# The second block's modulation summed on VectorE alone, with a seventh slot in the weight ring

## The chip, the cores and the metric

One Trainium2 chip, one core of it. The kernel is one launch; its time is the device time in microseconds (us) of that core, and the time of a kernel is the median of its runs.

## What is computed

A two-block network over 256 tokens of width 1024, all in float32. The first block has two layers, each of feed-forward, three attention branches and feed-forward; the second block has two layers with a Fourier or RWKV mixer and a mixture of 16 experts. Cut to what the change touches:

```
for l in range(2):                                   # first block
    x = x + 0.5 * swiglu(rmsnorm(x, g1[l]), w_ffn1_in[l], w_ffn1_out[l])
    x = x + merged_attention(x) @ w_out[l]
    x = x + 0.5 * swiglu(rmsnorm(x, g2[l]), w_ffn2_in[l], w_ffn2_out[l])
for i in range(2):                                   # second block
    mod_x   = silu(c)     @ ada_w[i] + ada_b[i]      # six parts of 1024 each
    mod_ctx = silu(c_ctx) @ ada_w[i] + ada_b[i]
    ... mixer(modulated x, ctx) ...; x = x + gate * ec_moe(modulated x)
```

The two modulation vectors depend on `c` and `c_ctx` alone, so the kernel computes them early, during the first block's feed-forward stages. `ada_w[i]` is 1024 x 6144: it is cut into three groups of 8 chunks of 128 x 2048.

## The kernel before

**The stream.** Nearly all weights are one stream of 632 chunks of 1 MB (128 partitions x 2048 float32, `CHUNK`), in the order of use. SyncE loads chunk c into slot c mod `RING` of the weight ring (`stream_weights`, L328 to L343). It loads a chunk as soon as the semaphore `chunks_used` says that the chunk `RING` places before it is used up; `RING` is 6. TensorE raises that semaphore after the last product with a chunk. ScalarE issues the other loads, some expert chunks among them ("kept" chunks, L2319).

**A feed-forward stage** (`ffn`, L601 on; four of them, stages 0, 2, 3 and 5). It has 33 weight chunks, numbered as pairs 0 to 32, each of two half-chunks i = 2 x pair and 2 x pair + 1. Half-chunks 0 to 43 are the up projection, in 11 groups of four; 44 (`UP`) to 65 are the down projection. For each half ScalarE rounds it to the high part (`round_half`, L644 to L650), VectorE subtracts to get the low part (`rest_half`, L652 to L655), and TensorE makes three products for each of two token tiles and two column blocks, 12 matmuls (L657 to L660). There are four split buffers, so half i is rounded once TensorE is done with half i - 4. After group n ScalarE applies SiLU, VectorE multiplies (`hid`, L877), TensorE transposes the result of the group before (`turn`, L693 to L702), ScalarE and VectorE save its high and low part (L830, L864). TensorE's order at the end of the up projection is: group 10, turn(9), halves 44 and 45 for token tile 1, turn(10), halves 44 and 45 for tile 0, then half by half. ScalarE's order there is: save(10), an activation table load (L853), then rounding of half 48 on.

**The modulation in these stages.** One group of `ada_w` for one stream (x or context) is weighed on VectorE: after each of the pairs 2, 4, ..., 16 the stream has one `ada` chunk, which VectorE multiplies by a column of silu(c) and adds to `partial_sums` (`weigh`, L672 to L682), in the program after the rest of half 2 x pair + 3. TensorE waits for that sum within the same half before it gives both chunks free (`follows_weighted`, `both_done`). At half UP + 15 `add_up` (L684 to L690) sums `partial_sums` over the partitions with four matmuls into bank 7. In stages 0, 2 and 3 a second group, for both streams at once, goes through TensorE: after pairs 25 and 29 the stream has four `ada` chunks, and `ada_chunk` (L1617 to L1623) makes four matmuls of 128 x 32 weights with each into bank 6. VectorE copies both banks out at half 64. In stage 0 GpSimd also places the attention bias (`place_bias`, L975 and L978).

**The expert stages** (`experts`, L1836 on; their products are L2103) follow a Fourier and an RWKV mixer. Each reads its own weights once, 16 experts of 12 chunks. Four chunks of an output projection (L1933) come before.

Of the kernel before, what the change touches and what calls it, by code (L numbers as in the profile page):

```python
# [17 lines left out]
F32 = mybir.dt.float32  # L18
F32R = mybir.dt.float32r
ALU = mybir.AluOpType  # L20
# [3 lines left out]
P = 128  # L24
# [9 lines left out]
CHUNK = 2048  # L34
RING = 6
HD = 64
# [24 lines left out]
class Signal:  # L61
# [10 lines left out]
    def dma(self):  # L72
        self.count += 16
        return self.sem, 16


# [107 lines left out]
class Program:  # L184
    def __init__(self, nc, io, ctx):
# [415 lines left out]
    def ffn(self, stage, second, ada=None, inner=None):  # L601
# [3 lines left out]
        with_bias = stage == 0  # L605
        split_fourth, hid_hi, hid_lo = self.scratch((CHUNK, F32R), (FT * SEQ, F32R), (FT * SEQ, F32R))
        hid_hi, hid_lo = (x[:, :].rearrange("p (k t) -> p k t", t=SEQ) for x in (hid_hi, hid_lo))
# [20 lines left out]

        group, stream = second
        weighted0, added0 = self.weighted.count, self.added_up.count  # L630

        def chunk_of(i):

            pair = i // 2
            return c0 + pair + min((pair - 1) // 2 if pair else 0, KT) + (min(max(pair - 2 * groups, 0) // 4 * 4, KT) if ada is not None else 0)

# [28 lines left out]
        def follows_weighted(i):  # L665
            return i % 4 == 3 and 7 <= i < 7 + 4 * KT

# [3 lines left out]

        def weigh(dve, k):  # L672
            self.wait_chunk(dve, chunk_of(4 * k + 7) - 1)
            if k == 0 and with_bias:
                dve.wait_ge(self.early["conditioned"].sem, 1)
            c, w = self.ada[:, 32 * k + stream:32 * k + stream + 1], self.slot(chunk_of(4 * k + 7) - 1)
            if k == 0:
                ins = dve.tensor_scalar(self.partial_sums[:, :], w, c, None, ALU.mult)
            else:
                dve.wait_ge(self.weighted.sem, weighted0 + k)  # L680
                ins = dve.scalar_tensor_tensor(out=self.partial_sums[:, :], in0=w, scalar=c, in1=self.partial_sums[:, :], op0=ALU.mult, op1=ALU.add)
            ins.then_inc(*self.weighted.up())  # L682

        def add_up(pe):  # L684
            pe.wait_ge(self.weighted.sem, weighted0 + KT)
            for j in range(4):
                last = pe.matmul(self.psum[32 * j:32 * j + 32, 7, :], self.pick[:, 1 - stream:33 - stream],
                                 self.partial_sums[:, j * NB:(j + 1) * NB], start=True, stop=True)
            last.then_inc(*self.added_up.up())

        @self.block.tensor
        def _(pe):
# [73 lines left out]
            for n in range(1, groups):  # L766
                if inner is not None:
                    inner.on_pe(pe, n - 1)
                if n >= 2:
                    pe.wait_ge(self.hid_done.sem, hid0 + n - 1)  # L770
                for i in range(4 * n, 4 * n + 4):
                    pe.wait_ge(self.rest.sem, rest0 + i + 1)
                    last = up(n, i, 0)
                    if follows_weighted(i):
                        pe.wait_ge(self.weighted.sem, weighted0 + n)
# [22 lines left out]
            for i in range(UP, N - 4):  # L798
                if i >= UP + AHEAD:
                    pe.wait_ge(self.rest.sem, rest0 + i + 1)  # L800
                    hidden(i)
                last = down(i, 0)
                if i >= UP + AHEAD:
                    last = down(i, 1)
                half_done(last, i)
                k = (i - UP) // 2
                if ada is not None and i == UP:
                    pe.wait_ge(self.early["conditioned"].sem, 1)
# [50 lines left out]
        def _(dve):  # L859
# [24 lines left out]
            for i in range(UP + 4, N):  # L884
                rest_half(dve, i)
                if i == N - 2:
                    dve.wait_ge(self.added_up.sem, added0 + 1)
# [5 lines left out]
                if ada is not None and i == N - 2:  # L893
                    dve.wait_ge(self.chunks_used.sem, chunk_of(UP + 2 * KT - 1) + 2)
                    dve.tensor_copy(self.ada_saved[ada], self.psum[:, 6, :]).then_inc(*ve.up())
# [719 lines left out]
    MOD = 34064  # L1615

    def ada_chunk(self, pe, chunk, k, cT, bank):  # L1617

        self.wait_chunk(pe, chunk)
        for j in range(4):  # L1620
            last = pe.matmul(self.psum[32 * j:32 * j + 32, bank, :], cT[:, k * 32:(k + 1) * 32],
                             self.slot(chunk)[:, j * NB:(j + 1) * NB], start=(k == 0), stop=(k == KT - 1))
        last.then_inc(*self.chunks_used.up())  # L1623

# [2096 lines left out]
def _stream(i):  # L3721
    parts = []
    ada = [_ada(i["ada_w_2"][l])[KT * g:KT * (g + 1)] for l in range(DEPTH) for g in range(3)]

    def up(w, group):
        for n, chunk in enumerate(_gate_up(w)):
# [4 lines left out]
    def down(w, group=None):  # L3731
        rows = list(_row_pairs(w))
        extra = [] if group is None else [ada[group][k - 3:k + 1] if k % 4 == 3 else ada[group][0:0] for k in range(KT)]
        for n, row in enumerate(rows):
            parts.append(row[None])
            parts.extend(extra[n:n + 1])

    for l in range(DEPTH):
        up(i["w_ffn1_in"][l], 5 if l else 4)
        down(i["w_ffn1_out"][l], 2 if l else 0)  # L3740
        parts += _mixer(i["w_in"][l], i["w_branch"][l], i["w_out"][l])
        up(i["w_ffn2_in"][l], 3)
        down(i["w_ffn2_out"][l], None if l else 1)
    for l in range(DEPTH):
# [117 lines left out]
```

## Time and profile before

| | us |
|---|---|
| three timed runs | 2948.0, 2947.13, 2941.61 |
| their median | 2947.13 |
| the profiled execution | 2939.34 |
| its span (first to last instruction) | 2937.5 |
| TensorE busy in the span | 2689.6 (92%) |
| VectorE busy | 1266.6 (43%) |
| ScalarE busy | 983.0 (33%) |
| mean DMA rate over the span | 244 GB/s |

The stretches of the span, in order: stage 0 to about 214 us, the attention stage, stage 2 from about 465, stage 3 from about 660, attention, stage 5 from about 1110 to 1300; the Fourier mixer to 1395; the first expert stage to about 1875; RWKV to about 2430; the second expert stage to the end. An engine's busy share says nothing alone: read for each stretch what is busy all through it, and what the engine next to finish last waits for. TensorE's ends in the profile are modelled; where two matmuls overlap in the timeline, the difference of their starts is the time that one takes.

### The profile page before, as it was taken

The numbers are of one execution on the slowest core, as the hardware profiler recorded it, in microseconds if no ns is written. First come the engines' busy times: TensorE is split into PE (matmuls) and PEld (weight loads), VectorE is DVE, ScalarE is ACT, GpSimd is POOL, SyncE is SP. The second block draws the span as 40 slices with busy tenths as digits, with TensorE's granted clock in tenths as the row PEclk, the third lists the DMA queues.
The fourth block names the chain that finished last, engine by engine and source line by source line (L and its number), as shares of the span: only waits on it lengthen the run. The fifth ranks groups of instructions, "written<-read, shape, count | busy, mean of one in ns | idle before, by whom it ended". The sixth has DMA issues, their size and how long they took to land. (4 is left out here: it accounts for less than half of the span.)

```text
span 2937.5 us, 56637 instructions
## 1 busy us (share of the span) xinstructions
PE 2689.6 (92%) x24326; PEld 1793.2 (61%) x24326; DVE 1266.6 (43%) x1829; ACT 983.0 (33%) x1704; POOL 189.1 (6%) x195
## 2 busy tenths in 40 slices
PE   8999999999999999999999998899999989776676
PEld 6877877878878878875433332344788864333332
DVE  5646566647556567643100001423777763000001
ACT  4435655434446555531200100202555542000000
POOL 0102000000002000000000000002343310000000
PEclk9999999999999999999999999999999989977777
DMA  7674335776673347633899999822000007999998
GB/s 302 244 283 163 126 131 213 269 287 244 247 283 129 129 163 274 229 136 113 347 421 421 421 421 421 331 85 74 33 17 11 11 21 305 421 421 421 417 421 337
DMA packets 103709, 715.43 MB, mean 244 GB/s; under 512 B 11916, under 2 KB 14348, under 8 KB 19512
## 3 DMA queue, kind: packets, MB, share of 16 engines
q1 hardware_dynamic: 93592, 667.94, 57.5%
q10 hardware_dynamic: 9888, 44.04, 4.0%
q8 instruction: 192, 3.15, 0.4%
q14 instruction: 37, 0.30, 0.0%
HBM read 710.86 MB, written 1.07 MB: 242 GB/s over the span
## 5 line engine op out<-in xcount | busy, mean ns | idle before, releaser
L2103 PE MATMUL banks<-weight_ring,scratch 128*32 128x256 f32 (+1 forms) x4304 | 567.1, 508 | 144.4 <-DMA weight_ring<-in_stream 142.7
L2103 PEld LDWEIGHTS banks<-weight_ring,scratch 128*32 128x32 f32 (+1 forms) x4304 | 185.9, 129 | 505.8 <-DMA weight_ring<-in_stream 252.7
L655 DVE TENSOR_TENSOR split_high<-weight_ring,split_high 128x1024 fp32r<-128x1024 f32 x198 | 244.5, 1243 | 207.6 <-ACT split_high L650 204.9
L650 ACT CAST split_high<-weight_ring 128x1024 fp32r<-128x1024 f32 x198 | 206.9, 1052 | 290.4 <-PE banks L660 218.7
L2254 DVE TENSOR_TENSOR scratch<-scratch,banks 128x512 f32<-128x512 f32 (+1 forms) x32 | 17.7, 554 | 570.4 <-PE banks L2103 570.4
L1433 DVE TENSOR_TENSOR split_high<-weight_ring,split_high 128x1024 fp32r<-128x1024 f32 x128 | 160.2, 1263 | 160.9 <-ACT split_high L1326 160.7
L658 PE MATMUL banks<-split_high,features_low 128*128 128x512 f32 x480 | 189.8, 395 | 0.0
L660 PE MATMUL banks<-split_high,features_high 128*128 128x512 f32 x480 | 187.1, 390 | 0.0
L659 PE MATMUL banks<-split_high,features_high 128*128 128x512 f32 x480 | 186.8, 389 | 0.0
L1326 ACT CAST split_high<-weight_ring 128x1024 fp32r<-128x1024 f32 x128 | 133.0, 1049 | 150.2 <-PE banks L1075 144.3
L2163 ACT ACTIVATE scratch<-banks 128x512 f32<-128x512 f32 (+1 forms) x32 | 15.7, 490 | 474.3 <-PE banks L2103 474.3
L1073 PE MATMUL banks<-split_high,features_low 128*128 128x512 f32 x392 | 156.6, 399 | 0.3
L1075 PE MATMUL banks<-split_high,features_high 128*128 128x512 f32 x392 | 152.9, 390 | 0.0
L1074 PE MATMUL banks<-split_high,features_high 128*128 128x512 f32 x392 | 152.9, 390 | 0.0
L2165 ACT COPY scratch<-banks 128x512 f32<-128x512 f32 (+1 forms) x32 | 15.3, 479 | 339.5 <-PE banks L2076 339.5
L655 DVE TENSOR_TENSOR scratch<-weight_ring,scratch 128x1024 fp32r<-128x1024 f32 x66 | 80.7, 1223 | 79.6 <-ACT scratch L650 79.1
L658 PE MATMUL banks<-split_high,scratch 128*128 128x512 f32 x264 | 103.6, 392 | 0.0
L660 PE MATMUL banks<-split_high,scratch 128*128 128x512 f32 x264 | 102.8, 389 | 0.0
L659 PE MATMUL banks<-split_high,scratch 128*128 128x512 f32 x264 | 102.7, 389 | 0.0
L650 ACT CAST scratch<-weight_ring 128x1024 fp32r<-128x1024 f32 x66 | 69.5, 1052 | 97.4 <-PE banks L660 59.7
L659 PEld LDWEIGHTS banks<-split_high,features_high 128*128 128x128 f32 x480 | 90.2, 188 | 19.0
L658 PEld LDWEIGHTS banks<-split_high,features_low 128*128 128x128 f32 x480 | 90.1, 188 | 18.9
(438 smaller groups left out, 4748.8 us busy)
## 6 DMA issues: line engine op xcount, KB each, us to landing
weight_ring<-in_stream SPq DMA_DIRECT2D x632, 1024.0 KB, 10.3
scratch<-in_kept ACTq DMA_DIRECT2D x20, 1024.0 KB, 9.6
scratch<-in_pair_rows ACTq DMA_DIRECT2D x8, 448.0 KB, 3.7
scratch<-in_kept ACTq DMA_DIRECT2D x6, 512.0 KB, 6.9
scratch<-in_lora ACTq DMA_DIRECT2D x2, 1536.0 KB, 8.4
front<-in_gain_rows ACTq DMA_DIRECT2D x5, 512.0 KB, 3.7
bias<-bias_rows SPq DMA_DIRECT2D x1, 2304.0 KB
scratch<-in_routing ACTq DMA_DIRECT2D x1, 1040.5 KB, 5.0
```

Source lines behind the costliest of these rows:

```text
L650: act.copy(split[i % 4][0], source(i)).then_inc(*self.rounded.up())
L655: dve.tensor_tensor(lo, source(i), hi.bitcast(F32), ALU.subtract).then_inc(*self.rest.up())
L658: pe.matmul(out, lhs_lo, hi, start=start, stop=False)
L659: pe.matmul(out, lhs_hi, lo, start=False, stop=False)
L660: return pe.matmul(out, lhs_hi, hi, start=False, stop=stop)
L1073: pe.matmul(out, lhs_lo, hi, start=start, stop=False)
L1074: pe.matmul(out, lhs_hi, lo, start=False, stop=False)
L1075: return pe.matmul(out, lhs_hi, hi, start=False, stop=stop)
L1326: act.copy(split[i % 3][0], source(i)).then_inc(*self.rounded.up())
L1433: dve.tensor_tensor(lo, source(i), hi.bitcast(F32), ALU.subtract).then_inc(*self.rest.up())
L2103: last = pe.matmul(self.psum[q * M:(q + 1) * M, (GATE, UP, DOWN)[part], 0:W], left, w[j][:, q * W:(q + 1) * W], start=(k == 0), stop=(k == ...
L2254: dve.tensor_tensor(hid[:, e % 2, 0:W], silu[:, e % 2, 0:W], self.psum[:, UP, 0:W], ALU.mult).then_inc(*up("hid"))
```

## The change

All three groups that went through TensorE are now weighed on VectorE too. In stages 0, 2 and 3 the stream has one chunk of that group after each of the pairs in `OWN_AT`: 13, 17, 19, 21 (up projection) and 23, 24, 26, 28 (down projection), and no bursts of four. For each, `weigh` makes two sums, one for each stream, one in the first half of `front` and one in the upper half of `resid`. `add_up` sums all three over the partitions (12 matmuls in these stages, 4 in stage 5), and stands after half 61 in all four stages instead of half 59. TensorE waits for the weighed sums in the middle of an up half and ahead of a down half. `partial_sums` moves into the stage's scratch, `flip` into a part of `ada`; the ring has seven slots; the Pool queue's scratch for dynamic DMAs goes from 1024 to 256 bytes.

```diff
-RING = 6
+RING = 7
+OWN_AT = (13, 17, 19, 21, 23, 24, 26, 28)
-        self.partial_sums = self.last.enter_context(nc.sbuf_tensor("partial_sums", [P, CHUNK], F32))
-        self.flip = self.resid[:, 3584:3712]
+        self.flip = self.ada[:, 1280:1408]
...
+        own_sums = [(self.front[:, 0:CHUNK], 0), (self.resid[:, 2 * D:4 * D], 1)]
+        weighted_at = {2 + 2 * k: (k, [(partial_sums[:, :], stream)]) for k in range(KT)}
+        if ada is not None:
+            weighted_at |= {place: (k, own_sums) for k, place in enumerate(OWN_AT)}
...
         def follows_weighted(i):
-            return i % 4 == 3 and 7 <= i < 7 + 4 * KT
+            return i % 2 == 1 and i // 2 - 1 in weighted_at
+
+        def weighted_by(i):
+            return weighted0 + sum(len(sums) for place, (_, sums) in weighted_at.items() if place < i // 2)
...
+            if k:
+                dve.wait_ge(self.weighted.sem, self.weighted.count)
+            for total, s in sums:
+                c, w = self.ada[:, 32 * k + s:32 * k + s + 1], self.slot(chunk)
+                if k == 0:
+                    ins = dve.tensor_scalar(total, w, c, None, ALU.mult)
+                else:
+                    ins = dve.scalar_tensor_tensor(out=total, in0=w, scalar=c, in1=total, op0=ALU.mult, op1=ALU.add)
+                ins.then_inc(*self.weighted.up())
 
         def add_up(pe):
-            pe.wait_ge(self.weighted.sem, weighted0 + KT)
+            pe.wait_ge(self.weighted.sem, weighted_by(N))
...
+            if ada is not None:
+                for total, s in own_sums:
+                    for j in range(4):
+                        out, cols = slice(32 * j, 32 * j + 32), slice(j * NB, (j + 1) * NB)
+                        last = pe.matmul(self.psum[out, 6, :], self.pick[:, 1 - s:33 - s], total[:, cols], start=(s == 0), stop=(s == 1))
...
+                if follows_weighted(i):
+                    pe.wait_ge(self.weighted.sem, weighted_by(i))
                 last = down(i, 0)
...
-                if ada is not None and i % 2 == 1 and k % 4 == 3 and k < KT:
-                    for j in range(4):
-                        self.ada_chunk(pe, chunk_of(i) + 1 + j, k - 3 + j, self.ada, 6)
-                if i == UP + 2 * KT - 1:
-                    add_up(pe)
+            add_up(pe)
...
                     rest_half(dve, i)
-                if n < KT:
-                    weigh(dve, n)
+                    if follows_weighted(i):
+                        weigh(dve, i)
...
-    nc = bacc.Bacc("TRN2", target_bir_lowering=False, num_devices=1, dynamic_dma_scratch_size=1024)
+    nc = bacc.Bacc("TRN2", target_bir_lowering=False, num_devices=1, dynamic_dma_scratch_size=256)
```

## Rows read from the trace of the kernel before

**Rows 1.** Page, parts 2, 3 and 4: rate in 40 slices, queues, chain.
```profile
GB/s 302 244 283 163 126 131 213 269 287 244 247 283 129 129 163 274 229 136 113 347 421 421 421 421 421 331 85 74 33 17 11 11 21 305 421 421 421 417 421 337
...
q1 hardware_dynamic: 93592, 667.94, 57.5%
q10 hardware_dynamic: 9888, 44.04, 4.0%
...
DMA 12%; PE 4%; DVE 1%; ACT 0%; issue 0%; SPq 0%; ACTq 0%; DVEq 0%
```

**Rows 2.** Windows: stretch, length, busy us (xcount) by engine, clock, DMA share, GB/s.
```profile
1395.00:1840.00 445.00, 413.82 (x2034) 155.17 (x2034) 47.44 (x105) 45.46 (x102) 0.00 (x0) 0.99 0.99 409
2430.00:2937.50 507.50, 371.64 (x3740) 174.99 (x3738) 51.81 (x127) 38.82 (x89) 0.00 (x0) 0.82 0.96 395
```

**Rows 3.** Windows of 10 us where both expert stages' first products begin.
```profile
1410.00:1420.00 10.00, 10.00 (x70) 8.76 (x70) 1.47 (x8) 5.08 (x14) 0.00 (x0) 0.83 0.47 138
...
2480.00:2490.00 10.00, 8.87 (x112) 6.53 (x116) 2.13 (x7) 4.71 (x10) 0.00 (x0) 1.00 0.23 77
```

**Rows 4.** Timeline of TensorE, first feed-forward stage: start, length, instructions.
```profile
173.61 0.39 PE L660 MATMUL banks<-scratch,scratch 128*128 128x512 f32 x1
173.92 3.64 PE L1621 MATMUL banks<-weight_ring,ada 128*32 128x512 f32 x32
177.50 0.50 PE L658 MATMUL banks<-split_high,scratch 128*128 128x512 f32 x1
...
199.16 0.39 PE L660 MATMUL banks<-scratch,scratch 128*128 128x512 f32 x1
...
202.94 1.04 PE L687 MATMUL banks<-partial_sums,small 128*32 128x512 f32 x8
203.91 0.50 PE L658 MATMUL banks<-split_high,scratch 128*128 128x512 f32 x1
```

**Rows 5.** Timeline of TensorE, fourth feed-forward stage, around its L687.
```profile
1273.66 0.39 PE L660 MATMUL banks<-split_high,scratch 128*128 128x512 f32 x1
...
1274.98 0.50 PE L658 MATMUL banks<-scratch,scratch 128*128 128x512 f32 x1
```

**Rows 6.** Instructions of L681: min/median/max ns, first and last start.
```profile
L681 DVE SCALAR_TENSOR_TENSOR partial_sums<-weight_ring,ada,partial_sums x28: 2342/2344/2347, 43.6 to 1196.8; 128x2048 f32<-128x2048 f32 x28
```

**Rows 7.** Timeline of VectorE, first feed-forward stage, its last two groups.
```profile
142.15 0.68 DVE L877 TENSOR_TENSOR front<-front,banks 128x512 f32<-128x512 f32 x1
...
146.94 1.23 DVE L655 TENSOR_TENSOR split_high<-weight_ring,split_high 128x1024 fp32r<-128x1024 f32 x1 [1.49 <-ACT split_high L650]
...
153.52 0.68 DVE L877 TENSOR_TENSOR front<-front,banks 128x512 f32<-128x512 f32 x1
```

**Rows 8.** Timeline of TensorE, same stage: the transposes of the last group.
```profile
154.29 0.62 PE L701 MATMUL banks<-ident,front 128*128 128x128 f32 x4
```

**Rows 9.** Timeline of ScalarE, same stage, after its last group.
```profile
155.55 1.28 ACT L853 ACT_TABLE_LOAD   x1
```

**Rows 10.** Timeline of VectorE, same stage: rests of half-chunks 48 to 51.
```profile
158.02 2.36 DVE L655 TENSOR_TENSOR split_high<-weight_ring,split_high 128x1024 fp32r<-128x1024 f32 x2 [1.77 <-ACT split_high L650]
...
161.52 1.23 DVE L655 TENSOR_TENSOR split_high<-weight_ring,split_high 128x1024 fp32r<-128x1024 f32 x1 [1.14 <-ACT split_high L650]
164.24 1.23 DVE L655 TENSOR_TENSOR scratch<-weight_ring,scratch 128x1024 fp32r<-128x1024 f32 x1 [1.49 <-ACT scratch L650]
```

**Rows 11.** Timeline of GpSimd, first feed-forward stage.
```profile
118.90 4.26 POOL L975 TENSOR_SCALAR_AFFINE_SELECT bias<-bias 128x3072 f32<-128x3072 f32 x1 [118.47 <-ACT bias L963]
123.31 3.60 POOL L978 TENSOR_SCALAR_AFFINE_SELECT bias<-bias 128x3072 f32<-128x3072 f32 x1
```

**Rows 12.** Timeline of VectorE over the same time.
```profile
118.16 2.34 DVE L681 SCALAR_TENSOR_TENSOR partial_sums<-weight_ring,ada,partial_sums 128x2048 f32<-128x2048 f32 x1
120.43 0.68 DVE L877 TENSOR_TENSOR front<-front,banks 128x512 f32<-128x512 f32 x1
...
121.63 7.49 DVE L655 TENSOR_TENSOR split_high<-weight_ring,split_high 128x1024 fp32r<-128x1024 f32 x3
```

More of the change, by code:

```diff
@@ L605, in ffn @@
         with_bias = stage == 0
-        split_fourth, hid_hi, hid_lo = self.scratch((CHUNK, F32R), (FT * SEQ, F32R), (FT * SEQ, F32R))
+        split_fourth, hid_hi, hid_lo, partial_sums = self.scratch((CHUNK, F32R), (FT * SEQ, F32R), (FT * SEQ, F32R), (CHUNK, F32))
         hid_hi, hid_lo = (x[:, :].rearrange("p (k t) -> p k t", t=SEQ) for x in (hid_hi, hid_lo))
@@ L634, in chunk_of @@
             pair = i // 2
-            return c0 + pair + min((pair - 1) // 2 if pair else 0, KT) + (min(max(pair - 2 * groups, 0) // 4 * 4, KT) if ada is not None else 0)
+            return c0 + pair + sum(place < pair for place in weighted_at)
         def used(i):
@@ L670, in both_done, with weigh @@
             ins.then_inc(self.chunks_used.sem, 2)
-        def weigh(dve, k):
-            self.wait_chunk(dve, chunk_of(4 * k + 7) - 1)
+        def weigh(dve, i):
+            k, sums = weighted_at[i // 2 - 1]
+            chunk = chunk_of(i) - 1
+            self.wait_chunk(dve, chunk)
             if k == 0 and with_bias:
[L675 to L682, printed above, removed]
+                if sums is own_sums:
+                    dve.wait_ge(self.bias_moved.sem, self.bias_moved.count)
+                else:
+                    dve.wait_ge(self.early["conditioned"].sem, 1)
+            if k:
[4 more added lines that the diff above has]
+                    ins = dve.tensor_scalar(total, w, c, None, ALU.mult)
+                else:
+                    ins = dve.scalar_tensor_tensor(out=total, in0=w, scalar=c, in1=total, op0=ALU.mult, op1=ALU.add)
+                ins.then_inc(*self.weighted.up())
@@ L684, in add_up @@
         def add_up(pe):
-            pe.wait_ge(self.weighted.sem, weighted0 + KT)
+            pe.wait_ge(self.weighted.sem, weighted_by(N))
             for j in range(4):
-                last = pe.matmul(self.psum[32 * j:32 * j + 32, 7, :], self.pick[:, 1 - stream:33 - stream],
-                                 self.partial_sums[:, j * NB:(j + 1) * NB], start=True, stop=True)
+                out, cols = slice(32 * j, 32 * j + 32), slice(j * NB, (j + 1) * NB)
+                last = pe.matmul(self.psum[out, 7, :], self.pick[:, 1 - stream:33 - stream], partial_sums[:, cols], start=True, stop=True)
@@ L801, in _ @@
                     hidden(i)
+                if follows_weighted(i):
+                    pe.wait_ge(self.weighted.sem, weighted_by(i))
                 last = down(i, 0)
@@ L804, in _ @@
                     last = down(i, 1)
[L805 to L808, printed above, removed]
-                if ada is not None and i % 2 == 1 and k % 4 == 3 and k < KT:
-                    for j in range(4):
-                        self.ada_chunk(pe, chunk_of(i) + 1 + j, k - 3 + j, self.ada, 6)
-                if i == UP + 2 * KT - 1:
-                    add_up(pe)
+                if follows_weighted(i):
+                    both_done(last)
+                else:
+                    half_done(last, i)
+            add_up(pe)
             for t in range(TT):
@@ L870, in _ @@
                     rest_half(dve, i)
-                if n < KT:
-                    weigh(dve, n)
+                    if follows_weighted(i):
+                        weigh(dve, i)
                 dve.wait_ge(self.act_done.sem, act0 + n + 1)
@@ L885, in _ @@
                 rest_half(dve, i)
+                if follows_weighted(i):
+                    weigh(dve, i)
                 if i == N - 2:
@@ L1615 @@
     MOD = 34064
[L1617 to L1623, printed above, removed]
     def copy_mod(self, dve, g, bank):
@@ L3723, in _stream, with feed @@
     ada = [_ada(i["ada_w_2"][l])[KT * g:KT * (g + 1)] for l in range(DEPTH) for g in range(3)]
-    def up(w, group):
-        for n, chunk in enumerate(_gate_up(w)):
+    def feed(w_in, w_out, group, own=None):
+        for n, chunk in enumerate([*_gate_up(w_in), *_row_pairs(w_out)]):
             parts.append(chunk[None])
@@ L3729, in up @@
                 parts.append(ada[group][n // 2 - 1:n // 2])
[L3731 to L3736, printed above, removed]
+            if own is not None and n in OWN_AT:
+                k = OWN_AT.index(n)
+                parts.append(ada[own][k:k + 1])
     for l in range(DEPTH):
-        up(i["w_ffn1_in"][l], 5 if l else 4)
-        down(i["w_ffn1_out"][l], 2 if l else 0)
+        feed(i["w_ffn1_in"][l], i["w_ffn1_out"][l], 5 if l else 4, 2 if l else 0)
         parts += _mixer(i["w_in"][l], i["w_branch"][l], i["w_out"][l])
-        up(i["w_ffn2_in"][l], 3)
-        down(i["w_ffn2_out"][l], None if l else 1)
+        feed(i["w_ffn2_in"][l], i["w_ffn2_out"][l], 3, None if l else 1)
     for l in range(DEPTH):
```

3 lines of the change are left out of this document (1 added, 2 removed).

## Prediction

> **What bounds the kernel now.** I read the page's chain and queues first, then the time by stretch, then the timelines where the edit acts. The chain of waits that ended last gives 12% of the span to DMA and 4% to TensorE [rows 1]; it reaches back only to the entry of the second expert stage, and so tells of that alone. The windows by stretch say the rest. In both expert stages the DMA engines are busy for 0.99 and 0.96 of the time at about 409 and 395 GB/s, while TensorE has idle time: 31 of 445 us and 136 of 507 us [rows 2]. There the weight stream sets the end. In the feed-forward stages it is the other way round. One matmul follows another without a gap in TensorE's timeline, the bursts included [rows 4], and the edit touches exactly these two kinds of stretch: matmuls in the one, prefetch in the other.
>
> **Part 1, the removed bursts.** In stages 0, 2 and 3, `ada_chunk` runs twice, four chunks at a time. The first burst is 32 records in 3.64 us, and the time that it really costs is the distance between the normal products around it: 177.50 - 173.61 = 3.89, less the 0.23 that lies between two such products anyway (12 of them in a half of 2.72 us, [rows 10]), so 3.66 us. The second burst with `add_up` behind it costs 203.91 - 199.16 - 0.23 = 4.52 [rows 4]. Together 8.18 us of TensorE time per stage, none of it beside other TensorE work, so all on the path.
>
> **Part 2, the larger `add_up`.** Where it stands alone, in stage 5, the old one of 4 matmuls costs 1274.98 - 1273.66 - 0.23 = 1.09 us [rows 5]; behind a burst, 203.91 - 202.94 = 0.97 [rows 4]. A set of four that follows others costs what the second burst takes beyond the first, 4.52 - 3.66 = 0.86. New price 1.09 + 2 x 0.86 = 2.81. So per stage 8.18 - 2.81 = 5.37 us less on TensorE. In stage 5 it only moves by two halves: nothing.
>
> **Part 3, the weighing.** A sum costs 2344 ns, and all 28 of them lie within 5 ns [rows 6]; the next instruction starts 2.27 us after it [rows 12]. One own chunk is 4.54 us on VectorE (in the first of each stage the sums are plain products, and shorter). In all 3 x 15 x 2.3 = some 105 us are added to VectorE, and TensorE shows none of it as long as each lies within the lead that the four split buffers give. That lead: TensorE takes 2.72 us for a half (rests 50 and 51 start at 161.52 and 164.24, [rows 10]). Half 51 ends at 173.84, where the burst begins [rows 4], so half 47 ended four halves earlier, at 162.96, and rest 51 started 1.28 us later. A rest ends 2.5 us after half i - 4 is done, while half i is wanted 3 x 2.72 = 8.16 us after. A rest then has 5.7 us to spare, and a weighing of 4.54 us in front of the wait for it leaves some 1.1 us. So single weighings (halves 29, 37, 41, 55, 59) are hidden, in the down projection barely; in the up projection TensorE waits half a half later (1.4 us more). Two places aren't like that.
>
> *The turn of the last group.* The chunk after pair 21 is weighed after rest 45. Rest 45 starts at 146.94, so the sums end at 146.94 + 1.14 + 4.54 = 152.62; rests 46 and 47 follow at 1.14 each (both have been rounded by then), and the product `hid` of group 10 starts at 154.90 instead of 153.52 [rows 7]. It takes 0.68 and a semaphore, so turn(10) can start at about 155.65. It starts at 154.29 now, right at the end of the present product: it has no slack [rows 8]. TensorE's order is fixed, so it waits: **1.36 us** per stage, three times.
>
> *Two chunks in a row.* The chunks after pairs 23 and 24 are weighed after rests 49 and 51. ScalarE's table load (now at 155.55, [rows 9]) moves with turn(10) by 1.36, and so do rests 48 and 49, which now start at 158.02 [rows 10]. VectorE then runs without a gap: rests 48, 49 from 159.38, sums to 166.2, rests 50, 51 to 168.5, sums to 173.1. TensorE wants the first pair of sums when half 48 is done, at 167.0 (162.96 + 2.72 + 1.36), which holds by 0.7, and the second when half 50 is, at 172.5: it waits **0.7 us**. After that each weighing has 1.1 us to spare again.
>
> Per stage 5.37 - 1.36 - 0.7 = 3.3, times three 9.8 us. Behind TensorE's new waits stand only its own next halves; behind VectorE's sums stand the rests, counted above. The chunk to be weighed lies in the stream ahead of the chunk whose rest was just made, so waiting for it costs nothing. The copies of banks 6 and 7 at half 64 wait for `add_up` after half 61: counted from the end of half 60 they end at 2.72 + 2.81 + 1.2 = 6.7 us, and rest 65 at 7.9; it is wanted at 5.53 + 3 x 1.36 = 9.6. Hidden by 1.7 us.
>
> **Part 4, GpSimd in stage 0.** While its two selects run, from 118.90 to 126.9 [rows 11], three rests that take 3.5 us elsewhere take 7.49 [rows 12]: 4 us lost. The own chunk after pair 17 is weighed right behind them. VectorE's work in a group of four is then 4 x 1.14 + 2 x 0.6 + 4.54 = 10.3 us against 11.37 for TensorE (142.15 to 153.52, [rows 7]), so it makes up about 1.07 a group; of the lateness about 0.5 us is left at turn(10). The bounds are 0 and 2 us. I take 0.5, so 9.3 for the stages. The Trainium skill (SBUF — State Buffer, section Who interferes with whom) says that a VectorE instruction with two SBUF inputs and a GpSimd one that reads SBUF exclude each other, whoever starts first. The trace agrees with it for the rests. By that rule the change would lose up to 7.9 us here if its sums fell on the selects; by the order of the rows they fall behind them, so the 0.5 stays.
>
> **Part 5, the seventh slot.** A chunk is 1.05 MB, and at 421 GB/s, the rate of the full slices, takes 2.49 us [rows 1]. At the start of the experts' products the ring is full and the DMA engines partly idle, 0.47 and 0.23 busy [rows 3], and later never again. So with seven slots one chunk more is in place when the stream becomes the bound, and the stage ends one transfer earlier: 2.49 us each, 5.0 together. It can't be more from this, since DMA has no gap left to fill after that; it can be nothing if TensorE, 93% busy in the first expert stage [rows 2], is its real bound. In the feed-forward stages the slot covers the denser stretch (pairs 12 to 17 and 21 to 28), where a half-pair of 5.4 us uses two chunks that take 5.0 to load: no gain, it keeps the supply.
>
> **Parts at nothing.** The scratch for dynamic DMAs: both busy queues are hardware ones, issued by SyncE and ScalarE [rows 1], none by GpSimd. The first seven loads delay the bias round trip on SyncE by one transfer, 2.5 us; the bias is first used in the third group, two groups of 11.37 us later. The moved buffers change no size.
>
> **Sum.** 9.3 + 5.0 = 14.3 us. Span 2937.5 to 2923.2, the profiled execution 2939.3 to 2925.0. The median of the runs lies 7.8 above that execution; against it the forecast is 2947.1 - 14.3 = **2932.8 us**.
>
> **Rivals.**
>
> *The two waits don't come* (the last product and turn have slack that I don't see, or a rest and a sum overlap more). Then 3 x 5.37 + 5.0 = 21.1: 2926.0. Against it: turn(10) starts now the moment `hid` is there. Chance 0.15.
>
> *The seventh slot gives nothing*, TensorE being the bound of the first expert stage and the second refilling as before: 9.3 alone, 2937.8. For it is 93% busy; against it the DMA rate without a dip. Chance 0.15.
>
> *VectorE is tighter than the rows add up to.* With 1.2 us more at turn(10) and at each of the weighings 49, 51, 55 and 59 (semaphores, a rounding that comes late because its chunk does) the stages lose 1.2 + 0.5 + 1.2 + 0.1 + 0.1 = 3.1 each, and give nothing: only the 5.0 of the ring is left, 2942.1. The lead of 1.1 us is small enough for it. Chance 0.15.
>
> *Slower: the weighing becomes the bound of the down projection.* Its place is halves 48 to 59, where VectorE has 4 x 2 sums and 12 rests: 8 x 2.27 + 12 x 1.14 = 31.8 us against 12 x 2.72 = 32.6 of TensorE. The point is 0.8 us: whatever VectorE needs beyond the rows there goes into the end. At 2.27 us a sum it holds; with a sum at 3.4 us, half as long again (a second operand from a slot that is being written, say), it's 8 x 1.1 - 0.8 = 8.2 more, and 2 more at turn(10), with 1.1 x 2 in each up-group that has no room: about 12 per stage, 36 - 14.3 = 22 slower: 2969; slower at all from a sum of 2.8 us. The 28 sums within 5 ns, all beside running loads, speak against it. Chance 0.07.
>
> The forecast as it stands has 0.48.
>
> **Range and chances.** The forecast with its own bounds (0 to 2 us for GpSimd, 0.5 us per wait, the scatter of the median, 6.4 us between the runs of before) is 2927 to 2939. To hold 8 in 10 it must take in the first rival and most of the third: 2923 to 2945. About 0.2% (5.9 us) is what a measurement of this kernel can tell from no change, so faster is below 2941.2. Forecast, first and second rival lie there but for the scatter, and a third of the third: 0.76. Same 0.16, slower 0.08.
>
> **What would show it.** In the profile after: no L1621; 24 matmul records at `add_up` within about 2.8 us; 45 sums more at 2.34 us; a wait of TensorE of about 1.4 us for L877's successor ahead of the last turn and of 0.7 us ahead of half 51, in each of three stages, and none at halves 55 and 59; the Fourier stage starting 9 us earlier, and each expert stage shorter by 2.5. If the waits are absent, part 3 was wrong about the lead; if the expert stages keep their length, part 5 was.

## The result and the profile after

| | before | after |
|---|---|---|
| median of the runs shown together | 2941.47 (2937.47 to 2948.0, 6 runs) | 2928.41 (2919.31 to 2930.3, 6 runs) |
| ratio after/before | | 0.9940, 95% interval 0.9927 to 0.9953 |
| the profiled execution | 2939.34 | 2928.78 |
| its span | 2937.5 | 2927.0 |

The changed kernel is faster: by 13 us if the two medians are subtracted, by 14 to 21 us if the interval of the ratio is taken. The forecast was 14.3 us. The ratio, here and below, is the one on record for each comparison, with its 95% interval. It isn't the quotient of the medians shown, which is 0.9956 here; in all comparisons but one the ratio lies 0.0003 to 0.0016 below that quotient (with five slots they agree). So a gain read from a ratio and one read from medians differ by up to 5 us. Run once more beside other runs of before, the changed kernel stood at 0.9946. Its page, busy time and chain:

```profile
span 2927.0 us, 56413 instructions
PE 2669.4 (91%) x24182; PEld 1787.8 (61%) x24182; DVE 1365.9 (47%) x1877; ACT 984.8 (34%) x1704; POOL 188.9 (6%) x195
...
DMA 12%; PE 4%; DVE 0%; ACT 0%; issue 0%; SPq 0%; ACTq 0%
```

VectorE is busy for 99 us more, TensorE for 20 us less, and the chain hasn't changed: it tells of the last stage alone, as [rows 1] did.

TensorE's timeline in the first feed-forward stage of after. Where [rows 4] had two bursts, there is one run of `add_up`; the transposes of the last group, turn(10) (L721 was L701), and half 51 now wait:

```profile
150.72 0.60 PE L721 MATMUL banks<-ident,front 128*128 128x128 f32 x4
...
155.59 0.66 PE L721 MATMUL banks<-ident,front 128*128 128x128 f32 x4 [1.51 <-DVE front L895]
...
172.22 0.39 PE L665 MATMUL banks<-split_high,scratch 128*128 128x512 f32 x1
173.19 0.47 PE L663 MATMUL banks<-scratch,scratch 128*128 128x512 f32 x1 [0.58 <-DVE resid L696]
...
203.01 0.39 PE L665 MATMUL banks<-split_high,scratch 128*128 128x512 f32 x1
203.32 1.07 PE L703 MATMUL banks<-scratch,small 128*32 128x512 f32 x8
204.21 1.04 PE L708 MATMUL banks<-front,small 128*32 128x512 f32 x8
205.06 1.04 PE L708 MATMUL banks<-resid,small 128*32 128x512 f32 x8
206.04 0.50 PE L663 MATMUL banks<-split_high,scratch 128*128 128x512 f32 x1
```

The bracket is the idle time before the instruction and what ended it. VectorE's timeline says why (L660 is the rest, L696 the sum, L895 `hid`):

```profile
148.06 2.34 DVE L696 SCALAR_TENSOR_TENSOR front<-weight_ring,ada,front 128x2048 f32<-128x2048 f32 x1
150.33 2.33 DVE L696 SCALAR_TENSOR_TENSOR resid<-weight_ring,ada,resid 128x2048 f32<-128x2048 f32 x1
...
154.86 0.67 DVE L895 TENSOR_TENSOR front<-front,banks 128x512 f32<-128x512 f32 x1
...
168.43 2.35 DVE L696 SCALAR_TENSOR_TENSOR front<-weight_ring,ada,front 128x2048 f32<-128x2048 f32 x1
170.69 2.35 DVE L696 SCALAR_TENSOR_TENSOR resid<-weight_ring,ada,resid 128x2048 f32<-128x2048 f32 x1
```

`hid` starts at 154.86 (forecast 154.90), the turn at 155.59 (155.65), the second pair of sums ends at 173.04 (173.1).

TensorE's waits in the first 1300 us, for these two lines (us in total, times, longest):

```profile
PE banks L721 <- DVE front L895: 3.8, 3, 1.5
...
PE banks L663 <- DVE resid L696: 1.8, 3, 0.6
```

Once in each of the three stages, and nowhere else. And the windows of both expert stages, to be held against [rows 2]:

```profile
1395.00:1840.00 445.00, 415.14 (x2054) 154.44 (x2056) 43.26 (x88) 42.50 (x96) 0.00 (x0) 1.00 0.99 410
2430.00:2927.00 497.00, 360.35 (x3717) 169.14 (x3716) 49.65 (x117) 36.73 (x86) 0.00 (x0) 0.82 0.95 393
```

**Where the time went, by stretch.** A stage's length is the distance between marks in the trace: the first transposes of a stage for the feed-forward stages, the first and last start of the experts' products, and the first RWKV product to the first product of the next output projection. Stage 0 is taken from the turn of group 9, because the start of the program varies: its second set of transposes begins anywhere between 21.2 and 22.9 us from one kernel to the next. This isn't the edit, since the order with spread weighings shows 21.62 in one run and 21.22 in another. Two marks of after as they stand:

```profile
459.01 1.09 PE L597 MATMUL banks<-ident,front 128*128 128x128 f32 x8 [0.49 <-DVE front L567]
...
653.16 1.03 PE L597 MATMUL banks<-ident,front 128*128 128x128 f32 x8
```

All kernels, one profiled execution each (us, read to about 0.1):

| kernel | stage 0 from turn(9) | stage 2 | stage 3 | experts 1 | RWKV | experts 2 |
|---|---|---|---|---|---|---|
| before | 69.3 | 197.4 | 196.6 | 451.5 | 542.6 | 439.2 |
| after | 66.4 | 194.2 | 193.3 | 449.4 | 545.2 | 438.6 |
| after again | 66.3 | 194.1 | 193.3 | 451.2 | 542.9 | 437.1 |
| after, 6 slots | 66.6 | 194.1 | 193.3 | 451.3 | 544.0 | 440.8 |
| before, 7 slots | 69.3 | 197.4 | 196.6 | 450.6 | 543.6 | 438.0 |
| own sums left out | 63.8 | 191.9 | 191.2 | 449.1 | 545.8 | 437.8 |
| no pair | 65.5 | 193.3 | 192.5 | 449.4 | 540.6 | 438.3 |
| no turn wait | 64.6 | 192.8 | 192.0 | 449.6 | 547.4 | 437.4 |
| spread | 63.8 | 191.9 | 191.2 | 449.4 | 547.2 | 437.8 |
| spread again | 63.8 | 192.0 | 191.2 | 450.8 | 539.2 | 437.6 |
| spread, 6 slots | 63.8 | 193.1 | 193.6 | 452.9 | 541.5 | 440.7 |
| bunched | 74.0 | 201.9 | 201.1 | 449.2 | 545.3 | 438.4 |
| after, 5 slots | 69.6 | 202.2 | 199.9 | 457.8 | 539.1 | 442.8 |

Equal feed-forward stages repeat to 0.1 us, the expert stages to 2 us, the RWKV stage only to 8 us.

### The profile page after: what moved, and what is told of

It is laid out like the page before. It is cut to its first block and busy times, and to the rows that moved or that the text cites. A ratio compares the mean times of both kernels' runs of the same rounds, so it can differ in the third digit from the quotient of the medians.

```text
span 2927.0 us, 56413 instructions
## 1 busy us (share of the span) xinstructions
PE 2669.4 (91%) x24182; PEld 1787.8 (61%) x24182; DVE 1365.9 (47%) x1877; ACT 984.8 (34%) x1704; POOL 188.9 (6%) x195
## 5 line engine op out<-in xcount | busy, mean ns | idle before, releaser
L660 DVE TENSOR_TENSOR split_high<-weight_ring,split_high 128x1024 fp32r<-128x1024 f32 x198 | 243.7, 1241 | 124.7 <-ACT split_high L655 121.8
L2174 ACT ACTIVATE scratch<-banks 128x512 f32<-128x512 f32 (+1 forms) x32 | 15.7, 490 | 473.8 <-PE banks L2114 473.8
L2273 DVE TENSOR_TENSOR scratch<-banks,scratch 128x512 f32<-128x512 f32 (+1 forms) x32 | 17.9, 558 | 187.4 <-PE banks L2114 187.4
L664 PEld LDWEIGHTS banks<-split_high,features_high 128*128 128x128 f32 x480 | 90.2, 188 | 19.0
L665 PEld LDWEIGHTS banks<-split_high,features_high 128*128 128x128 f32 x480 | 90.1, 188 | 19.0
```

The costliest lines, as they stand in the source:

```text
L660: dve.tensor_tensor(lo, source(i), hi.bitcast(F32), ALU.subtract).then_inc(*self.rest.up())
L664: pe.matmul(out, lhs_hi, lo, start=False, stop=False)
L665: return pe.matmul(out, lhs_hi, hi, start=False, stop=stop)
```

## The experiments

Each edit is one to the changed kernel, unless it says otherwise.

**Six slots.**
```diff
-RING = 7
+RING = 6
```


> The changed kernel with the ring back at six slots, nothing else. Theory (seventh slot worth one transfer per expert stage, nothing in the feed-forward stages): the feed-forward stages keep their length to 0.3 us, each expert stage is 2.5 us longer from its first product to its last; 5 us longer than the changed kernel, so 8 to 10 us (0.3%) faster than before. Rival (the slot feeds the denser stream of the feed-forward stages): halves 48 to 60 wait for rounding, ScalarE shows waits for the ring, and most of the 9.6 us gained there goes. Second rival (the slot does nothing at all): the same time as the changed kernel.

Measured: 2929.97 us, ratio 0.9944 (0.9930 to 0.9957), span 2929.4. The ratio can't tell this from the changed kernel (0.9940 and 0.9946). The stages say more: stages 2 and 3 are as with seven slots, with the same two waits, and the expert stages are 451.3 and 440.8. In stages 2 and 3 of this order the seventh slot gives nothing. ScalarE waits for chunks again, and only in stage 0 does that reach TensorE, for 0.6 us in all. Waits in the first 1300 us, ScalarE's in the changed kernel:

```profile
ACT split_high L655 <- DMA weight_ring<-in_stream: 5.2, 3, 2.6
```

and ScalarE's and TensorE's with six slots:

```profile
ACT split_high L655 <- DMA weight_ring<-in_stream: 63.0, 22, 4.0
...
PE banks L721 <- DVE front L895: 4.0, 3, 1.7
...
PE banks L663 <- DVE resid L696: 1.8, 3, 0.6
```

In stage 0 a chunk comes late for ScalarE while GpSimd's selects hold VectorE up anyway. The rests and the two own sums behind them end later, TensorE's weight load in half 37 waits 0.6 for the second sum, and turn(9) comes 129.4 us after the second set of transposes instead of 129.0. The wait of turn(10) is 1.7 instead of 1.5. TensorE's weight loads, stage 0, with six slots:

```profile
132.43 0.19 PEld L663 LDWEIGHTS banks<-split_high,features_low 128*128 128x128 f32 x1 [0.57 <-DVE resid L696]
```

**The seventh slot alone**, in the kernel before, with the room that it needs.
```diff
-RING = 6
+RING = 7
-        self.partial_sums = self.last.enter_context(nc.sbuf_tensor("partial_sums", [P, CHUNK], F32))
-        split_fourth, hid_hi, hid_lo = self.scratch(...)
+        split_fourth, hid_hi, hid_lo, self.partial_sums = self.scratch(...)
-    ... dynamic_dma_scratch_size=1024)
+    ... dynamic_dma_scratch_size=256)
```


> The kernel before with seven slots, the sum buffer in the stage's scratch to make room, the bursts left as they are. Theory: 2 x 2.5 = 5.0 us faster than before (0.17%), all of it in the expert stages; TensorE's bursts of 3.66 and 4.52 us unchanged. In the profile of the changed kernel the second expert stage gave only 0.6 us from first product to last. Rival (the slot is worth 2.5 in the first expert stage and little in the second): 3 us. Rival (nothing): 0.

Measured: 2940.63 us, ratio 0.9981 (0.9971 to 0.9990), with feed-forward stages of 197.4 and 196.6 as before. The median is 3.0 us below that of before, the interval of the ratio says 3 to 8.5. So the slot is worth something by itself, and only behind the feed-forward stages; whether it is 5.0 or the rival's 3, this run doesn't decide.

**The weighings apart from each other and ahead of the turn.**
```diff
-OWN_AT = (13, 17, 19, 21, 23, 24, 26, 28)
+OWN_AT = (11, 13, 15, 19, 23, 25, 27, 29)
```


> The changed kernel with the own chunks after pairs 11, 13, 15, 19, 23, 25, 27, 29 in place of 13, 17, 19, 21, 23, 24, 26, 28: none is weighed right ahead of the last product, no two lie in neighbouring pairs of the down projection, and none right behind the two selects of GpSimd. Theory (the waits come from VectorE's lateness at those two places): the waits of TensorE for the last turn (1.4, 1.4 and 1.5 us) and ahead of half 51 (0.6 each) are gone in all three stages, and each feed-forward stage is 2.0 us shorter, 6 to 7 us in all; 19 us or 0.65% faster than before. Rival (VectorE as a whole is too full, so the wait comes out elsewhere): new waits of the same sum at other halves, the same time as the changed kernel.

Measured: 2918.99 us, ratio 0.9907 (0.9891 to 0.9922). Both waits are gone from TensorE's list. In the second feed-forward stage the last two turns stand 3.21 us apart, as in before; in after it was 591.73 - 587.21 = 4.52. First this kernel's timeline of TensorE:

```profile
584.75 0.60 PE L721 MATMUL banks<-ident,front 128*128 128x128 f32 x4
...
587.96 0.61 PE L721 MATMUL banks<-ident,front 128*128 128x128 f32 x4
```

then after's:

```profile
587.21 0.60 PE L721 MATMUL banks<-ident,front 128*128 128x128 f32 x4
...
591.73 0.66 PE L721 MATMUL banks<-ident,front 128*128 128x128 f32 x4 [1.17 <-DVE front L895]
```

The stages gain 5.5, 5.5 and 5.4 us on before, where parts 1 and 2 of the prediction gave 5.37 for TensorE's work alone. So the waits were all that stood between that and the 3.3 of the changed kernel.

**The weighings left out.** Seven of the eight weighings of the own group don't run, and the last is a plain product, so the modulation of these three groups isn't computed.
```diff
...
+            if sums is own_sums and k < KT - 1:
+                return
...
-                if k == 0:
+                if k == 0 or sums is own_sums:
```


> The changed kernel without seven of the eight own weighings of each stage: the chunks are loaded and given free as before, but only the last is weighed (a plain product), so the modulation of three groups comes out wrong. It prices the TensorE side alone. Theory: per stage 8.18 - 2.81 = 5.37 us less than before, 16.1 in all, with no wait of TensorE for VectorE; 21 us (0.7%) faster than before with the ring's 5. Rival (the gain on TensorE is smaller and the waits are not the reason): the same time as the changed kernel.

Measured: 2921.15 us, ratio 0.9912 (0.9898 to 0.9925). VectorE has 91 us less to do, and the stages are as long as in the spread order, to 0.1 us. In the spread order the whole weighing on VectorE costs these stages nothing; the 2.2 us between this median and that of the spread order are within the scatter of the RWKV stage.

**The changed kernel again.** No edit.

> The changed kernel once more, to see which stage lengths of its profile repeat. Theory: the seams of the feed-forward stages come back to 0.3 us (217.1, 653.2, 846.5), and the 2.6 us by which the RWKV stage was longer than before does not: it is scatter of that stage, which the edit doesn't touch. Rival (the seventh slot costs the RWKV stage something): its length is 545 us again, against 542.6 and 544.0 with six slots.

Measured: 2927.06 us, ratio 0.9946 (0.9925 to 0.9967), span 2924.1, 2.9 less than the first profile of the same kernel. Feed-forward stages and waits are the same; RWKV is 542.9 instead of 545.2, so the longer RWKV stage of the first profile doesn't repeat; expert stage 2 is 437.1 instead of 438.6 and expert stage 1 is 451.2 instead of 449.4.

**The pair apart, the turn as it was.**
```diff
+OWN_AT = (13, 17, 19, 21, 23, 25, 27, 29)
```


> Own chunks after pairs 13, 17, 19, 21, 23, 25, 27, 29: the two neighbouring ones of the down projection are taken apart, the one ahead of the last turn stays. Theory: TensorE's waits of 0.6 us ahead of half 51 go, its waits of 1.4 to 1.5 us ahead of the last turn stay, each feed-forward stage is 0.6 us shorter than in the changed kernel and 1.4 longer than with the spread places; some 16 us faster than before. Rival (both waits have one cause): both go.

Measured: 2923.44 us, ratio 0.9932 (0.9914 to 0.9951). No wait for a sum is left, the turn waits as before (3.8 us in three), and each stage is 0.8 to 0.9 shorter than in the changed kernel, a little more than the 0.6 expected. A recorded wait of 0.59 costs 0.83, since it is told from the end of the last matmul, while the next product could have started 0.16 ahead of that, and the first product after a stop takes 0.31 instead of 0.23 to make way for the next.

**The turn's weighings forward, the pair as it was.**
```diff
+OWN_AT = (11, 13, 15, 19, 23, 24, 26, 28)
```


> OWN_AT = (11, 13, 15, 19, 23, 24, 26, 28): only the own weighings ahead of the last group's turn are moved forward, the pair at rounds 23 and 24 stays. The other two kernels of this kind put the pair's price at 0.85 us a stage (stage 2 is 0.9 shorter without it) and the turn's at 1.35 (a further 1.4 without it). If the two waits are separate, this kernel has no wait ahead of the last turn, keeps 0.6 ahead of half 51, its second feed-forward stage is 192.8 us long (194.2 in the changed kernel, 191.9 with both gone), and it is 4 us faster than the changed kernel. The rival: the turn's wait holds the rest up and so shields half 51; then VectorE, which gets no slack from the turn, makes TensorE wait 1.5 us or more ahead of half 51, and nearly nothing is gained.

Measured: 2922.01 us, ratio 0.9929 (0.9916 to 0.9942). Stage 2 is 192.8, as expected, the wait ahead of half 51 is 0.6 in each stage, that of the turn is gone. The two waits are separate: 1.4 us and 0.9 us off stage 2, and 2.3 together.

**All in a bunch**, pairs 21 to 25 in a row.
```diff
+OWN_AT = (13, 17, 19, 21, 22, 23, 24, 25)
```


> Own chunks after pairs 13, 17, 19, 21, 22, 23, 24, 25, so five weighings of 4.54 us in a row from half 45 to half 53. Theory by the lead (rest done 2.5 us after half i - 4, wanted after 8.16, 4.54 for each weighing): the last product comes another 4.5 us late, so TensorE waits 5.9 us for the last turn instead of 1.4, 0.7 ahead of half 51 and some 1.4 ahead of half 53; the three stages together are 17 to 18 us longer than in the changed kernel, which is 4 us slower than before. Rival (VectorE has more room than that, since waits overlap): under 8 us longer, and still faster than before.

Measured: 2948.63 us, ratio 1.0019 (1.0005 to 1.0033), slower than before, and 21.6 over the changed kernel instead of 17 to 18. The waits came near what was expected: 6.1, 5.7 and 5.7 at the turn, 0.2 ahead of half 51, 1.1 ahead of half 53. They are 21.3 us in all, 15.7 more than in the changed kernel, while the stages are longer by 7.6 to 7.8 each, 23 in all. Most of the rest is TensorE's clock. Timeline of TensorE right after the wait in stage 2:

```profile
604.56 1.12 PE L721 MATMUL banks<-ident,front 128*128 128x128 f32 x4 [5.69 <-DVE front L895]
605.33 0.78 PE L663 MATMUL banks<-scratch,scratch 128*128 128x512 f32 x1
605.90 0.63 PE L664 MATMUL banks<-scratch,scratch 128*128 128x512 f32 x1
606.33 0.63 PE L665 MATMUL banks<-scratch,scratch 128*128 128x512 f32 x1
...
608.89 0.56 PE L665 MATMUL banks<-split_high,scratch 128*128 128x512 f32 x1
609.28 0.40 PE L663 MATMUL banks<-split_high,scratch 128*128 128x512 f32 x1
```

and the windows over it (the number after POOL's is the granted clock, then the DMA share and GB/s):

```profile
600.00:604.50 4.50, 0.00 (x0) 0.00 (x0) 4.50 (x4) 0.00 (x0) 0.00 (x0) 0.77 0.02 7
604.50:607.00 2.50, 2.44 (x8) 2.15 (x9) 1.27 (x3) 1.27 (x2) 0.00 (x0) 0.50 0.10 20
607.00:609.00 2.00, 2.00 (x6) 1.52 (x6) 0.03 (x1) 1.53 (x3) 0.00 (x0) 0.50 0.67 238
609.00:611.00 2.00, 2.00 (x10) 1.64 (x9) 1.23 (x1) 1.14 (x2) 0.00 (x0) 0.94 0.00 0
```

Late in the wait the clock falls from 1.00 to 0.50, which is 1.2 GHz (0.77 in the mean of the last 4.5 us), and it stays low for some 4.5 us after the restart: products start 0.43 apart instead of 0.23. From 605.33 to 609.28 it is nine steps in 3.95 us instead of 0.31 + 8 x 0.227 = 2.13, and the transposes take 0.77 instead of 0.41. That is 2.2 us beyond the wait itself. In stages 0 and 3 the same stretch takes 2.1 and 2.4 longer than in the changed kernel, so it is 6.7 in three stages.

**Five slots.**
```diff
-RING = 7
+RING = 5
```


> The changed kernel with five slots. Theory: the expert stages lose another 1.9 to 2.5 us each (first to last product was 451.4 and 440.0 on average with six slots, 449.6 and 438.1 with seven), so 453.5 and 442; in the feed-forward stages five slots no longer cover the dense stretch, roundings wait for the ring and TensorE waits, about 11 us more in the three stages; together about 20 us over the changed kernel, 2 to 8 us slower than before. Rival (the prefetch depth doesn't matter as long as the mean rate holds): 4 us over the changed kernel, all in the expert stages.

Measured: 2962.35 us, ratio 1.0076 (1.0054 to 1.0097), 35 over the changed kernel instead of 20, and 22 over before. Stage 0 has lost 3.4 us already ahead of the turn of group 9 (it comes 132.4 us after the second set of transposes instead of 129.0) and 3.2 behind it; stages 2 and 3 are 8.0 and 6.6 longer, the experts' 457.8 and 442.8 (expected 453.5 and 442). The first expert stage has lost more than two transfers; why wasn't taken apart. ScalarE now waits for chunks in earnest, and it reaches TensorE through VectorE:

```profile
ACT split_high L655 <- DMA weight_ring<-in_stream: 210.2, 57, 8.3
...
PE banks L663 <- DVE resid L696: 8.7, 5, 2.7
PE banks L721 <- DVE front L895: 7.1, 3, 2.7
```

The expectation, 11 us, was half of the 21 that the feed-forward stages lost. TensorE's recorded waits for VectorE there are 14.5 us more than in the changed kernel, counting 4.3 in which it waits for a rest; the low clock after three of the waits (below) adds some 4.7.

**The spread order with six slots, and with seven once more.** Both have the `OWN_AT` of the spread order; the first has this beside it:
```diff
-RING = 7
+RING = 6
```


> OWN_AT = (11, 13, 15, 19, 23, 25, 27, 29) and RING = 6. If the seventh slot pays only in the expert stages, about 1.9 us each, as the changed kernel and the kernel before with six and seven slots say, this is 3.7 us slower than the same order with seven slots, and the feed-forward stages stay at 191.9 and 191.2 us. The rival: weighing from round 11 on means that VectorE frees the slots of the stream later ahead of half 33, and with one slot less chunks come late: a wait of some 0.6 us ahead of half 33 in every feed-forward stage and in the first, where GpSimd's work is late too, 1.8 more ahead of halves 36 and 37: then it is 7 us slower than with seven slots, and the seventh slot is what lets the weighings be spread.

> OWN_AT = (11, 13, 15, 19, 23, 25, 27, 29) with seven slots once more, beside the same order with six slots and beside the one that moves only the turn's weighings. Both theories expect it again at 0.991 of the kernel before, no wait of TensorE for a weighing in the feed-forward stages, and stages of 191.9 and 191.2 us. If the earlier run was luck of the first or the last stages, it comes out by 3 us or more elsewhere, with the two stage lengths unchanged.

Measured side by side: 2925.93 us with six slots, 0.9944 (0.9930 to 0.9958), and 2916.94 with seven, 0.9914 (0.9901 to 0.9927). The spread order repeats. Here the slot is worth 9 us, and the stage lengths say of what: 1.1 and 2.4 in stages 2 and 3, 2.1 and 3.1 in the expert stages, together 8.7. It is more than either expectation gave (3.7 and 7). The rival's wait in half 33 is there in stages 2 and 3 (0.8 and 0.9), in stage 3 with one of 1.0 in half 29 before it; stage 0 lost nothing, against that rival. TensorE's timeline, stage 2, with six slots:

```profile
554.20 0.39 PE L665 MATMUL banks<-split_high,features_high 128*128 128x512 f32 x1
555.42 0.50 PE L663 MATMUL banks<-split_high,features_low 128*128 128x512 f32 x1 [0.83 <-DVE resid L696]
```

Part of what this order gains it can only hold with the seventh slot.

## Why the prediction was right, point by point

**Parts 1 and 2, TensorE's work** were right. The new `add_up` costs 206.04 - 203.01 - 0.23 = 2.80 us (forecast 2.81), and the order without waits gains 5.4 to 5.5 a stage (5.37).

**Part 3, the two waits** came in their places and nowhere else. VectorE has 42 sums more at 2.34 us and six plain products at 1.28, not the 45 sums of the prediction, which changes its total by under 1 us. The turn waits 1.51 us in stage 0 and 1.17 in stage 2; by the distance of the turns it costs 1.66 and 1.31 (forecast 1.36, plus GpSimd's part in stage 0). Half 51 waits 0.59 and costs 0.83 (0.7). Halves 55 and 59 and the copies at half 64 show no wait. Stages 2 and 3 gain 3.2 and 3.3, forecast 3.3. Each wait taken away alone gave its own share back, and both together the sum.

**Part 4, GpSimd in stage 0**: 0.5 was taken; the turn waits 1.51 - 1.17 = 0.34 longer than in stage 2, where GpSimd doesn't work. The reason given fits: VectorE runs without a gap from the selects to the product of group 10, and a group with an own chunk takes it 10.27 and 10.26 us (144.60 - 134.33 and 154.86 - 144.60; forecast 10.3), where TensorE's takes 11.37. VectorE's timeline in after while the selects run, here from 118.53 to 126.5, and the products of groups 8 and 9:

```profile
121.25 6.36 DVE L660 TENSOR_TENSOR split_high<-weight_ring,split_high 128x1024 fp32r<-128x1024 f32 x2
127.54 2.34 DVE L696 SCALAR_TENSOR_TENSOR front<-weight_ring,ada,front 128x2048 f32<-128x2048 f32 x1
...
134.33 0.67 DVE L895 TENSOR_TENSOR front<-front,banks 128x512 f32<-128x512 f32 x1
...
144.60 0.67 DVE L895 TENSOR_TENSOR front<-front,banks 128x512 f32<-128x512 f32 x1
```

Two rests take 6.36 us instead of 2.36, and the first sum behind them its normal 2.34. A sum that had started before the selects, at 117.79, kept its 2.34 too. The Trainium skill (SBUF — State Buffer, section Who interferes with whom) states the exclusion; the trace agrees for the rests, and the sums of the change lie behind the selects.

**Part 5, the seventh slot** was right in its mechanism and a little too large in size: 5.0 forecast, 4.3 measured. The mechanism can be counted in the traces. When the first product of the two expert stages starts, 263 and 461 chunks of the stream have landed in every kernel with seven slots, 262 and 460 with six, 261 and 459 with five: one chunk more for each slot. Over the three kernels with six slots the expert stages are 451.9 and 440.2 on average, over the nine with seven 449.9 and 437.9: 2.0 and 2.3 us, against one transfer of 2.49. In the single pair of before and after the second stage shows only 0.6 of it, and the forecast that each stage gets 2.5 shorter would have looked wrong there; after has a dip in the DMA rate there that before hasn't, and kernels that are alike in this differ by 1.8 and 2.6 (last section). Below six slots the price isn't one transfer: from six to five the first expert stage loses 5.9 us. That the slot gives nothing in the feed-forward stages held for stages 2 and 3 of the order as changed; in its stage 0 the slot gives 0.6 us, and in stages 2 and 3 of the spread order 3.5.

**The sum.** Up to the first product of the output projection behind the Fourier mixer (L1933, now L1944) the two profiles differ by 1329.6 - 1320.0 = 9.6 us (forecast 9.3; the start of the program gave 0.4 of it). The expert stages add 2.1 and 0.6, the Fourier and router part 1.0 (from the start of stage 5 to the experts' first product the 13 profiles range over 1.7), and the RWKV stage takes 2.6 back: 10.5 in the spans. The forecast had no term for that last, and shouldn't have: over 13 profiles that all run the same code in it, it is between 539.1 and 547.4 long. It is most of why the gain in the span of one profile falls 3.8 short of the forecast, while the medians of two separate comparisons give 13.1 and 13.0. The terms of the feed-forward stages can be read to 0.1 us, the whole can't: a gain of 13 by the medians and one of 14 to 21 by the ratio both stand beside the 14.3.

**The base.** The median of before was 2947.13 in the runs that the prediction had, and 2940 to 2944 in every later set. So 2932.8 is 4.4 above the measured 2928.4, though by the medians the gain was forecast 1.2 too large. The reason lies in the three runs, not in a step.

**The rivals.** That the waits don't come is refuted by the two brackets. That the slot gives nothing is refuted by the kernel before with seven slots. VectorE isn't tighter than its rows: with the weighing left out nothing but the two waits is gained. The weighing didn't become the bound of the down projection, since its sums kept their length. Instructions of the sum's line in after (min/median/max ns, first and last start):

```profile
L696 DVE SCALAR_TENSOR_TENSOR front<-weight_ring,ada,front x21: 2336/2346/2349, 127.5 to 818.8; 128x2048 f32<-128x2048 f32 x21
```

The bunched order shows what longer waits would have done: the clock adds to them, for which that rival had no term.

## What to carry to other kernels

Work moved to an engine that is busy half of the time is free only where each piece fits in the lead that the buffers give; look for the places where two pieces meet, or where a piece stands ahead of an instruction without slack, and move those. Here an edit of one tuple did it, worth 7.0 us in three stages: from 0.9940 and 0.9946 of before to 0.9907 and 0.9914. To see a few microseconds, measure the stages between marks in the trace, since one stage that the edit doesn't touch may scatter by more than the edit is worth.

## What the hardware showed that was not expected

A wait of TensorE isn't priced by its length alone. After waits of 1.2 to 1.5 us the clock stayed at 1.00. After waits of 5.7 us it was 0.50 for some 4.5 us, which adds 2.1 to 2.4. In between it isn't only the length: the kernel with five slots has five waits of 2.06 to 2.74 us, and three of them (2.06, 2.64, 2.74) were followed by the low clock, two (2.09, 2.74) were not. At the two turns among the three it adds about 1.5 us each. Windows right behind a wait of 2.64 us ahead of the last turn of stage 2, and behind one of 2.74 us ahead of a down half 20 us later:

```profile
602.30:604.00 1.70, 1.64 (x6) 1.54 (x7) 0.61 (x2) 0.48 (x1) 0.00 (x0) 0.50 0.00 0
...
623.70:626.00 2.30, 2.21 (x10) 1.85 (x11) 2.22 (x2) 0.27 (x1) 0.00 (x0) 1.00 0.53 224
```

What makes the difference was not tried.

Second, filling the ring at the start of the second expert stage. The first product starts at 2476.06 in after. In windows of 2 us from 2480 on, the rate (last number) is

```profile
2480.00:2482.00 2.00, 2.00 (x44) 1.23 (x40) 0.00 (x0) 0.17 (x1) 0.00 (x0) 1.00 1.10 373
2482.00:2484.00 2.00, 2.00 (x32) 1.33 (x25) 0.42 (x1) 0.00 (x0) 0.00 (x0) 1.00 0.88 307
2484.00:2486.00 2.00, 2.00 (x21) 1.27 (x23) 0.42 (x1) 1.08 (x3) 0.00 (x0) 1.00 0.92 377
2486.00:2488.00 2.00, 2.00 (x44) 1.22 (x40) 0.48 (x1) 0.00 (x0) 0.00 (x0) 1.00 1.03 434
```

Before and the second run of the changed kernel show no such dip: 422 and 430, 426 and 426 GB/s in the two windows in question, 4 to 8 us after the first product, where after has 348 and 311. It loses about one microsecond of transfer. Of the ten others, seven have the dip, the kernel before with seven slots among them (344 and 295), and three don't. So it isn't the edit. It goes with a longer stage: with seven slots 437.8 to 438.6 us with the dip and 437.1 to 437.6 without, with six slots 440.7 to 440.8 and 439.2. Like compared with like, by the means, the seventh slot gives 2.6 and 1.8 us there. What the dip is was not tried.
